# Row projections that start with a pair of chunks, 512 columns wide, split by the inner dimension

## The chip, the cores and the metric

The kernel runs on one core of a Trainium2 chip. A core has a matrix engine (TensorE, "PE" in the rows; its loads of the stationary operand are "PEld"), VectorE ("DVE"), ScalarE ("ACT"), GpSimd ("POOL") and SyncE ("SP"), which issues the transfers. Each engine runs its own list of instructions in order and waits on semaphores. The metric is the device time of one execution in microseconds (us); the time of the kernel before is the median of three runs.

## The reference, cut to what matters

Two transformer blocks follow one another on 256 rows of width 1024. The first block is applied for two layers, and each layer begins with a projection of the normed rows; a second one closes the attention. The second block has a cross attention whose output is projected in the same way.

```
for l in range(DEPTH):                      # 2 layers
    proj = h @ w_in[l]                      # (256 x 1024) @ (1024 x 1536)
    ... two attentions -> oa, ob ...
    mix = jnp.concatenate([oa, ob], axis=-1) @ w_o[l]      # 1024 x 1024
    h = layer_norm(DEEPNORM_ALPHA * h + mix, ln1_g[l], ln1_b[l])
    h = layer_norm(DEEPNORM_ALPHA * h + peer_ffn(h, ...), ...)
# second block: ... cross attention, its output @ w_o_x, rmsnorm, residual ...
```

So there are five such projections: w_in and w_o of layer 0, w_in and w_o of layer 1, and w_o_x. All data is float32.

## The kernel before, in words

**How a product is computed.** A float32 product is made of three products of rounded parts: high x high, high x low and low x high. The rows (the stationary operand) are turned by TensorE in two tiles of 128 rows (t = 0, 1), in eight blocks of 128 of the inner dimension each; ScalarE copies the turned tile from PSUM rounded to `xh` (the highs of the rows), and VectorE subtracts that copy to get `xl` (the lows). The copies are made by halves of a tile, four inner blocks each: `xh_half[t][i]` says that half i of tile t is there.

**Chunks.** A weight matrix comes in chunks of 256 columns with all 1024 rows, 1 MB each. SyncE loads them into the two places of `ring` in turn; a place is free again when both engines that read it have said so (`chunk_free`). A chunk has four quarters q; in the kernel before a quarter holds two inner blocks of 256 columns. ScalarE makes the high part of a quarter (`high`, L1415, into `wh`), once TensorE has left that quarter of `wh` (`parts_free[q]`). GpSimd makes the low parts of quarters 0 to 2 (`low`, L510, into `wl`), VectorE that of quarter 3 (`low`, L2103). `parts_ready[q]` tells TensorE.

**The start of a projection.** `to_xT` (L702) turns tile 0, computes some products whose result nobody reads (`spin`, L700, and `spin_on_weights`, L709, which keep the engine busy), turns tile 1, and spins again. `first_rows` (L743) then computes chunk 0: all high x high products first (16 matmuls of 256 columns, L752), then quarter by quarter the others (32 matmuls, L762). `rows_by_chunk` (L817) computes chunk 1 and the later ones, 12 matmuls of 256 columns (L829) per quarter, 48 per chunk; the last chunk of w_o and w_o_x is computed tile by tile (`rows_by_tile`, L839). Chunks alternate between two PSUM slots of two banks each, one bank per tile.

**The other engines.** ScalarE's list at a start is: the four highs of chunk 0, the four half copies of the turned tiles (`halves_to_xT`, L1493), then the highs of chunk 1 and so on. VectorE's list is: the four lows of the rows (`halves_low_xT`, L2137), `low(0, 3)`, and then for each chunk its low quarter and the taking of the result: a copy for w_in (L2212), a scaled add to the residual with statistics for w_o (L2342, L2346), a copy with sums of squares and a product with the gain for w_o_x (`residual_rows`, L1994, L1967, L2006). The kernel is one hand-written list per engine; nothing reorders it. Chunk 2 is loaded by `stream` (L313) once place 0 of the ring is free.

Of the kernel before, what the change touches and what calls it, by code (L numbers as in the profile page):

```python
# [8 lines left out]
P = 128  # L9
# [4 lines left out]
TT = S // P  # L14
HD = 64
CW = 256
CHUNK = KB * CW
N_IN, N_O, N_WQ = 6, 4, 8
# [24 lines left out]
def build(nc, A, out):  # L43
# [4 lines left out]
    with ctx:  # L48
# [633 lines left out]
        def _(pe):  # L682
# [60 lines left out]
            def first_rows(full):  # L743

                pe.wait_ge(slot_free[0], 1)
                pe.sem_inc(slot_free[0], -1)
                for t in range(TT):
                    for q in range(4):
                        if q % 2 == 0:
                            xh_in(t, q // 2)  # L750
                        for k in range(2):
                            pe.matmul(PS[:, t, 0:CW], xh[:, 2 * q + k, t * P:(t + 1) * P],  # L752
                                      wh[:, q, k * CW:(k + 1) * CW], start=q + k == 0, stop=False)
                for q in range(4):
                    if q % 2 == 0:
                        xl_in(q // 2)
                    pe.wait_ge(parts_ready[q], 1)
                    pe.sem_inc(parts_ready[q], -1)
                    for t in range(TT):
                        for k in range(2):  # L760
                            for i, (x, w) in enumerate(((xl, wh), (xh, wl))):
                                last = pe.matmul(PS[:, t, 0:CW], x[:, 2 * q + k, t * P:(t + 1) * P],  # L762
                                                 w[:, q, k * CW:(k + 1) * CW], start=False, stop=q + k + i == 5)
                    if q < 3:
                        last.then_inc(parts_free[q], 1)
                last.then_inc(full[0], 1)
# [219 lines left out]
            for l in range(DEPTH):  # L986

                to_xT(h, 11 if l else 0, 5 if l else 0, between=1 if l else 0, last=2 if l else 0)
# [13 lines left out]
                chunks(N_IN - 2, first_rows, rows_by_chunk, dve_full)  # L1002
# [847 lines left out]
        def _(dve):  # L1850
# [133 lines left out]
            def residual_rows(at, after, apart=False):  # L1984
# [11 lines left out]
                for c in range(3):  # L1996
# [204 lines left out]
            for l in range(DEPTH):  # L2201
# [4 lines left out]

                def take_proj(c):
                    at = (3 + c) % N_IN * CW
                    if 0 < c < 4:
                        low(c % 2, 3)  # L2210
# [9 lines left out]
                for c in range(3):  # L2220
                    take_proj(c)
# [835 lines left out]
```

## Time and profile before

| | |
|---|---|
| median of 3 runs | 2506.39 us (2502.34 to 2509.07) |
| the profiled execution | 2505.94 us, its span 2504.1 us |
| TensorE busy | 2412.5 us (96%) |
| VectorE busy | 1748.9 us (70%) |
| ScalarE busy | 1343.7 us (54%) |
| GpSimd busy | 709.0 us (28%) |
| mean granted TensorE clock | 0.994 |

Busy time of TensorE is counted with overlapping matmuls, so the share says that something is nearly always in the array, not that it runs at its peak. The waits that matter are short, some tenths of a microsecond each, and stand in the timeline of a few starts and ends of projections. The five starts lie at 16, 130, 1016, 1129 and 2261 us.

### The profile page before, as it was taken

Reading aid. Unit: us, or ns where it says so; the run is one execution under the profiler, and the core shown is the slowest. Engines: PE = TensorE matmul, PEld = TensorE weight load, DVE = VectorE, ACT = ScalarE, POOL = GpSimd, SP = SyncE. Lnnn points to the kernel's source line nnn. Section 1 sums busy time; section 2 is a strip of 40 time slices with the busy share of each in tenths; the row PEclk is TensorE's granted clock in tenths of the full one; section 3 lists DMA queues with packets and bytes.
Section 4 is the critical chain, followed back from the end, with each engine's and each line's share of the span. In section 5 each row is a group of like instructions: output and inputs, shape, how many; then the busy total and the mean of one; then the engine's idle time right before and its main releaser. Section 6 shows DMA issues by size and latency. Waiting matters only on the chain. (4 is left out here: it accounts for less than half of the span.)

```text
span 2504.1 us, 57329 instructions
## 1 busy us (share of the span) xinstructions
PE 2412.5 (96%) x16509; PEld 2211.3 (88%) x16509; DVE 1748.9 (70%) x3945; ACT 1343.7 (54%) x2396; POOL 709.0 (28%) x564
## 2 busy tenths in 40 slices
PE   6999999999999999999999999999999999899998
PEld 6899999999888888889999999988888887688996
DVE  5647777887677777554777788777777767556346
ACT  3545555776555555454555567655555543444443
POOL 5665444000000000566544400000000043134665
PEclk9999999999999999999999999999999999999999
DMA  6244566444566666623466644456666644333554
GB/s 239 85 153 168 210 230 226 168 152 180 177 245 236 246 236 243 237 85 137 167 217 225 228 164 161 174 182 241 241 241 242 243 157 158 142 135 110 174 186 152
DMA packets 98053, 475.31 MB, mean 190 GB/s; under 512 B 11808, under 2 KB 13344, under 8 KB 50720
## 3 DMA queue, kind: packets, MB, share of 16 engines
q1 hardware_dynamic: 97392, 472.91, 53.3%
q10 hardware_dynamic: 560, 1.19, 0.1%
q8 instruction: 46, 0.75, 0.1%
q14 instruction: 55, 0.45, 0.1%
HBM read 438.41 MB, written 35.65 MB: 189 GB/s over the span
## 5 line engine op out<-in xcount | busy, mean ns | idle before, releaser
L1415 ACT ACTIVATE wh<-ring 128x512 fp32r<-128x512 f32 x1428 | 881.9, 627 | 613.9 <-ACTq L1414 609.3
L2103 DVE TENSOR_TENSOR wl<-ring,wh 128x512 fp32r<-128x512 f32 x961 | 674.1, 707 | 273.0 <-DVEq L2102 254.2
L1100 PE MATMUL PS<-xh,wh 128*128 128x256 f32 x2048 | 593.6, 290 | 9.7 <-PEq L1096 8.2
L1100 PE MATMUL PS<-xl,wh 128*128 128x256 f32 x2048 | 579.6, 283 | 0.0
L1100 PE MATMUL PS<-xh,wl 128*128 128x256 f32 x2048 | 579.5, 283 | 0.0
L510 POOL TENSOR_TENSOR wl<-ring,wh 128x512 fp32r<-128x512 f32 x295 | 390.8, 1349 | 289.1 <-POOLq L509 287.3
L895 PE MATMUL PS<-wh,xh 128*128 128x512 f32 x1088 | 425.2, 391 | 2.5 <-PEq L892 2.5
L895 PE MATMUL PS<-wh,xl 128*128 128x512 f32 x1088 | 423.5, 389 | 0.0
L895 PE MATMUL PS<-wl,xh 128*128 128x512 f32 x1088 | 423.3, 389 | 0.0
L1100 PEld LDWEIGHTS PS<-xh,wh 128*128 128x128 f32 x2048 | 392.3, 192 | 15.3 <-issue 14.6
L1100 PEld LDWEIGHTS PS<-xl,wh 128*128 128x128 f32 x2048 | 392.9, 192 | 0.0
L1100 PEld LDWEIGHTS PS<-xh,wl 128*128 128x128 f32 x2048 | 392.3, 192 | 0.0
L496 POOL TENSOR_TENSOR rstd<-ve,mhalf 128x1 f32<-128x1 f32 (+3 forms) x30 | 31.2, 1039 | 1237.7 <-POOLq L495 1213.3
L636 POOL TENSOR_TENSOR wl<-ring,wh 128x512 fp32r<-128x512 f32 x144 | 205.7, 1430 | 230.4 <-POOLq L635 229.9
L895 PEld LDWEIGHTS PS<-wh,xh 128*128 128x128 f32 x1088 | 204.2, 188 | 49.3 <-issue 7.3
L895 PEld LDWEIGHTS PS<-wh,xl 128*128 128x128 f32 x1088 | 204.2, 188 | 42.7
L895 PEld LDWEIGHTS PS<-wl,xh 128*128 128x128 f32 x1088 | 204.3, 188 | 42.1 <-issue 0.5
L870 PE MATMUL PS<-xh,wh 128*128 128x256 f32 x688 | 196.9, 286 | 3.3 <-PEq L866 3.0
L870 PE MATMUL PS<-xl,wh 128*128 128x256 f32 x688 | 194.6, 283 | 0.0
L870 PE MATMUL PS<-xh,wl 128*128 128x256 f32 x688 | 194.5, 283 | 0.0
L1636 ACT ACTIVATE stg<-PS 128x256 f32<-128x256 f32 x256 | 97.9, 382 | 155.7 <-ACTq L1631 93.0
L1702 ACT ACTIVATE xh<-gains 128x256 fp32r<-128x256 f32 x248 | 103.6, 418 | 127.3 <-ACTq L1700 124.8
(339 smaller groups left out, 3826.5 us busy)
## 6 DMA issues: line engine op xcount, KB each, us to landing
ring<-in_peer_u SPq DMA_DIRECT2D x128, 1024.0 KB, 4.8
ring<-in_peer_v SPq DMA_DIRECT2D x128, 1024.0 KB, 4.8
acts<-stg SPq DMA_DIRECT2D x124, 256.0 KB, 2.1
gains<-acts SPq DMA_DIRECT2D x124, 256.0 KB, 4.9
ring<-in_w_in SPq DMA_DIRECT2D x24, 1024.0 KB, 4.9
ring<-in_w_gate_up SPq DMA_DIRECT2D x22, 1024.0 KB, 4.8
ring<-in_peer_wq SPq DMA_DIRECT2D x16, 1024.0 KB, 4.8
ring<-in_w_down SPq DMA_DIRECT2D x11, 1024.0 KB, 4.9
```

Source lines behind the costliest of these rows:

```text
L496: pool.tensor_tensor(rstd[:, at:at + n], ve[:, at:at + n], mhalf[:, :].to_broadcast([P, n]), ALU.pow).then_inc(rstd_ready, 1)
L510: part = pool.tensor_tensor(wl[:, q, :], ring[:, s, q * QW:(q + 1) * QW], wh[:, q, :].bitcast(F32), SUB)
L636: pool.tensor_tensor(wl[:, q, :], ring[:, s, q * QW:(q + 1) * QW], wh[:, q, :].bitcast(F32), SUB).then_inc(parts_ready[q] if q == 0 else p ...
L870: last = pe.matmul(PS[:, 2 * s + b, 0:S], w[:, q, k * CW + b * P:k * CW + (b + 1) * P], x[:, 2 * q + k, :], start=q + k + i == 0, stop=q + ...
L895: last = pe.matmul(acc[:, t, c * 512:(c + 1) * 512], (xh, xl)[x][:, at + j, t * P:(t + 1) * P], w[:, q, :], start=begin and j + i == 0, st ...
L1100: last = pe.matmul(PS[:, 2 * j, 0:S], w[:, q, k * P:(k + 1) * P], x[:, at, :], start=at + i == 0, stop=at + i == 9)
L1415: act.activation(wh[:, q, :], ring[:, s, q * QW:(q + 1) * QW], ACT.Copy).then_inc(high_ready[q], 1)
L1636: last = act.activation(stg[:, s, j * S:(j + 1) * S], PS[:, 2 * j, 0:S], ACT.Gelu)
L1702: act.activation(wst[0][:, j, :], buf[:, j * S:(j + 1) * S], ACT.Copy).then_inc(cast_ready[j], 1)
L2103: part = dve.tensor_tensor(wl[:, q, :], ring[:, s, q * QW:(q + 1) * QW], wh[:, q, :].bitcast(F32), SUB)
```

## The change

The first two chunks of the five projections become a pair. The host lays their weights out anew (`first_pair_wide`): the first chunk of the pair now holds inner blocks 0 to 3 with 512 columns, one block per quarter, the second chunk inner blocks 4 to 7. `wide_start` takes the place of `to_xT`, `first_rows` and `rows_by_chunk` for chunk 1. It writes 512 columns per tile into the slot 1.

```
+            def wide_start(src, idle=0, spins=(0, 0, 0), halves=True):
...
+                def highs(t):
+                    xh_in(t, 0)
+                    for q in range(4):
+                        pe.matmul(PS[:, 2 + t, :], xh[:, q, t * P:(t + 1) * P], wh[:, q, :], start=q == 0, stop=False)
...
+                turn(0, 0)
+                turn(0, 1)
+                pe.wait_ge(highs_in, 1)
...
+                spin_on_weights(spins[0])
+                pe.wait_ge(slot_free[1], 1)
...
+                highs(0)
+                spin_on_weights(spins[1])
...
+                turn(1, 0)
+                spin_on_weights(spins[2])
+                highs(1)
+                turn(1, 1)
...
                 for q in range(4):
...
+                        for x, w in ((xl, wh), (xh, wl)):
+                            last = pe.matmul(PS[:, 2 + t, :], x[:, q, t * P:(t + 1) * P], w[:, q, :], start=False,
+                                             stop=False)
+                    last.then_inc(parts_free[q], 1)
+                for t in range(TT):
+                    xh_in(t, 1)
+                    pe.wait_ge(slot_free[2 + t], 1)
+                for q in range(4):
...
+                        for i, (x, w) in enumerate(((xh, wh), (xh, wl), (xl, wh))):
+                            last = pe.matmul(PS[:, 2 + t, :], x[:, 4 + q, t * P:(t + 1) * P], w[:, q, :], start=False,
+                                             stop=q == 3 and i == 2)
...
-                to_xT(h, 11 if l else 0, 5 if l else 0, between=1 if l else 0, last=2 if l else 0)
+                wide_start(h, 11 if l else 0, (1, 1, 1) if l else (0, 0, 0))
...
-                to_xT(o_all, 14, 6, halves=False, last=2)
-                first_rows(dve_full)
-                rows_by_chunk(1, dve_full)
+                wide_start(o_all, 14, (1, 1, 1), False)
...
-            to_xT(o_all, 0, 2, halves=False, last=2)
-            first_rows(dve_full)
-            rows_by_chunk(1, dve_full)
+            wide_start(o_all, 0, (1, 0, 1), False)
```

VectorE takes the pair in one operation. For w_o the order of low and statistics changes too:

```
-                for i in range(3):
-                    s = i % 2
-                    if i:
-                        low(s, 3)
+                low(1, 3)
+                for s, lo, hi in ((1, 0, 2), (0, 2, 3)):
                     take_rows(s)
...
                     dve.sem_inc(slot_free[s], 1)
+                    low(1 - s, 3)
                     for t in range(TT):
-                        dve.bn_stats(stats4[:, t, i, :], h[:, t, c])
-                low(1, 3)
+                        for i in range(lo, hi):
+                            dve.bn_stats(stats4[:, t, i, :], h[:, t, CW * i:CW * (i + 1)])
```

For w_o_x the pair is copied (1024 columns in all), then come `low(0, 3)`, two sums of squares of 512 columns, and one product with the gain of 1024 columns; chunk 2 and the last one are taken as before. For w_in the pair is copied in one operation.

**What moves on TensorE, at the start of w_o.** The names: `ident` turns, `PS<-wh` alone is a spin, `wh,xh` is high x high. Before:

```order
L726 MATMUL PS<-ident,arena 128x128 [waits slot_free2,src_ready]
L726 MATMUL PS<-ident,arena 128x128 x7
L709 MATMUL PS<-wh 128x512 [waits highs_in,slot_free0]
L709 MATMUL PS<-wh 128x512 x5
L726 MATMUL PS<-ident,arena 128x128 [waits slot_free3,src_ready]
L726 MATMUL PS<-ident,arena 128x128 x7
L709 MATMUL PS<-wh 128x512 x2
L752 MATMUL PS<-wh,xh 128x256 [waits slot_free0,xh_half00]
L752 MATMUL PS<-wh,xh 128x256 x3
L752 MATMUL PS<-wh,xh 128x256 [waits xh_half01]
```

The same place in the changed kernel:

```order
L750 MATMUL PS<-ident,arena 128x128 x7
L761 MATMUL PS<-wh 128x512 [waits highs_in]
L757 MATMUL PS<-wh,xh 128x512 [waits slot_free1,xh_half00]
L757 MATMUL PS<-wh,xh 128x512 x3
L761 MATMUL PS<-wh 128x512
L750 MATMUL PS<-ident,arena 128x128 [waits slot_free3,src_ready]
L750 MATMUL PS<-ident,arena 128x128 x3
L761 MATMUL PS<-wh 128x512
L757 MATMUL PS<-wh,xh 128x512 [waits xh_half10]
L757 MATMUL PS<-wh,xh 128x512 x3
L750 MATMUL PS<-ident,arena 128x128 x4
L791 MATMUL PS<-wh,xl 128x512 [waits xl_half0,xl_half1,parts_ready0]
```

Four products of each tile now stand between the turns, and the second half of tile 1 is turned behind the products of its first half.

**What moves on VectorE, in w_o behind the start.** `L2342` and `L2392` add the result to the residual, `BN_STATS` are the statistics, `wl<-ring,wh` is the low quarter. Before, from chunk 1's low quarter to that of the last chunk:

```order
L2103 TENSOR_TENSOR wl<-ring,wh 128x512 [waits high_ready3]
L2342 SCALAR_TENSOR_TENSOR h<-h,PS 128x2x256 [waits dve_own,dve_full1]
L2346 BN_STATS stats<-h 128x6 [waits dve_own]
L2346 BN_STATS stats<-h 128x6
L2103 TENSOR_TENSOR wl<-ring,wh 128x512 [waits high_ready3]
L2342 SCALAR_TENSOR_TENSOR h<-h,PS 128x2x256 [waits dve_own,dve_full0]
L2346 BN_STATS stats<-h 128x6 [waits dve_own]
L2346 BN_STATS stats<-h 128x6
L2103 TENSOR_TENSOR wl<-ring,wh 128x512 [waits high_ready3]
```

In the changed kernel:

```order
L2152 TENSOR_TENSOR wl<-ring,wh 128x512 [waits dve_own,high_ready3]
L2392 SCALAR_TENSOR_TENSOR h<-h,PS 128x2x512 [waits dve_own,dve_full1]
L2152 TENSOR_TENSOR wl<-ring,wh 128x512 [waits dve_own,high_ready3]
L2398 BN_STATS stats<-h 128x6 [waits dve_own]
L2398 BN_STATS stats<-h 128x6 x3
L2392 SCALAR_TENSOR_TENSOR h<-h,PS 128x2x256 [waits dve_full0]
L2152 TENSOR_TENSOR wl<-ring,wh 128x512 [waits dve_own,high_ready3]
L2398 BN_STATS stats<-h 128x6 [waits dve_own]
```

The last chunk's low quarter now stands ahead of the statistics of chunk 2. On VectorE in w_o_x, from the pair's copy to the last chunk's low quarter, the changed kernel has:

```order
L2037 COPY arena<-PS 128x2x512 [waits dve_own,dve_full1]
L2152 TENSOR_TENSOR wl<-ring,wh 128x512 [waits dve_own,high_ready3]
L2004 ISA arena,stats<-arena 128x512 [waits dve_own]
L2004 ISA stats 128x1
L2042 MEMSET stats 128x1
L2004 ISA arena,stats<-arena 128x512
L2044 TENSOR_TENSOR arena<-arena,gains 128x2x512 [waits dve_own]
L2031 COPY arena<-PS 128x2x256 [waits dve_full0]
L2004 ISA arena,stats<-arena 128x256 [waits dve_own]
L2152 TENSOR_TENSOR wl<-ring,wh 128x512 [waits high_ready3]
```

Before, the work on chunk 0 was spread over the time in which chunk 1 was computed; now all of the pair's stands between the end of the pair and that of chunk 2. The order of instructions on ScalarE, GpSimd and SyncE is unchanged.

## Rows read from the trace of the kernel before

**Rows 1.** Page, part 1: busy time and its share of the span.

```profile
PE 2412.5 (96%) x16509; PEld 2211.3 (88%) x16509; DVE 1748.9 (70%) x3945; ACT 1343.7 (54%) x2396; POOL 709.0 (28%) x564
```

**Rows 2.** Timeline, TensorE, w_o of layer 0: start, duration, engine, line, operation, count.

```profile
136.22 0.28 PE L762 MATMUL PS<-wh,xl 128*128 128x256 f32 x1
...
140.06 0.29 PE L829 MATMUL PS<-wh,xh 128*128 128x256 f32 x1
```

**Rows 3.** Timeline, TensorE: 512 columns in the expert stage, 53 matmuls apart.

```profile
1929.79 0.39 PE L895 MATMUL PS<-wh,xl 128*128 128x512 f32 x1
...
1941.80 0.39 PE L895 MATMUL PS<-wl,xh 128*128 128x512 f32 x1
```

**Rows 4.** Timeline, TensorE, the start of w_o in layer 0.

```profile
132.93 1.07 PE L726 MATMUL PS<-ident,arena 128*128 128x128 f32 x8 [0.50 <-PEq L724]
...
134.30 2.08 PE L752 MATMUL PS<-wh,xh 128*128 128x256 f32 x16
```

**Rows 5.** Timeline, ScalarE, the same stretch.

```profile
130.73 1.09 ACT L1493 ACTIVATE xh<-PS 128x512 fp32r<-128x512 f32 x2 [2.10 <-ACTq L1492]
133.69 1.09 ACT L1493 ACTIVATE xh<-PS 128x512 fp32r<-128x512 f32 x2 [1.86 <-ACTq L1492]
137.47 0.63 ACT L1415 ACTIVATE wh<-ring 128x512 fp32r<-128x512 f32 x1 [2.69 <-ACTq L1414]
...
142.23 0.63 ACT L1415 ACTIVATE wh<-ring 128x512 fp32r<-128x512 f32 x1 [1.10 <-ACTq L1414]
```

**Rows 6.** Timelines, VectorE and GpSimd, the same stretch.

```profile
134.43 1.89 DVE L2137 TENSOR_TENSOR xl<-PS,xh 128x512 fp32r<-128x512 f32 x3 [1.04 <-PEq L733]
136.23 0.68 DVE L2103 TENSOR_TENSOR wl<-ring,wh 128x512 fp32r<-128x512 f32 x1
...
143.04 3.80 POOL L510 TENSOR_TENSOR wl<-ring,wh 128x512 fp32r<-128x512 f32 x3 [0.98 <-POOLq L509]
```

**Rows 7.** SyncE's issue of chunk 2, and its line's time to landing.

```profile
137.26 0.33 SPq L319 DMA_DIRECT2D ring<-in_w_o  x1
...
DMA to landing us min/median/max: 4.8/4.8/4.8
```

**Rows 8.** Timelines, VectorE and TensorE, the end of w_o in layer 0.

```profile
152.91 0.75 DVE L2346 BATCH_NORM_STATS2 stats<-h 128x6 f32<-128x256 f32 x2 [0.24 <-DVEq L1855]
153.58 0.67 DVE L2103 TENSOR_TENSOR wl<-ring,wh 128x512 fp32r<-128x512 f32 x1
...
154.55 0.36 PE L851 MATMUL PS<-wh,xh 128*128 128x256 f32 x1 [0.66 <-PEq L847]
```

**Rows 9.** Timeline, the start of w_in in layer 0.

```profile
21.45 2.88 PE L752 MATMUL PS<-wh,xh 128*128 128x256 f32 x16
...
24.16 0.28 PE L762 MATMUL PS<-wh,xl 128*128 128x256 f32 x1
...
24.81 11.70 SPq L319 DMA_DIRECT2D ring<-in_w_in  x3
```

**Rows 10.** Timeline, the start of w_in in layer 1.

```profile
1019.76 2.08 PE L752 MATMUL PS<-wh,xh 128*128 128x256 f32 x16
...
1019.12 4.25 POOL L510 TENSOR_TENSOR wl<-ring,wh 128x512 fp32r<-128x512 f32 x3 [2.91 <-POOLq L509]
...
1023.85 16.71 SPq L319 DMA_DIRECT2D ring<-in_w_in  x4
```

**Rows 11.** Timeline, w_o_x: its start on TensorE and ScalarE, its last low quarter on VectorE.

```profile
2262.63 1.06 PE L726 MATMUL PS<-ident,arena 128*128 128x128 f32 x8
...
2261.75 1.09 ACT L1493 ACTIVATE xh<-PS 128x512 fp32r<-128x512 f32 x2 [1.22 <-ACTq L1492]
...
2283.46 0.68 DVE L2103 TENSOR_TENSOR wl<-ring,wh 128x512 fp32r<-128x512 f32 x1
```

**Rows 12.** One line of the kernel: product with the gain; duration ns min/median/max.

```profile
L2006 DVE TENSOR_TENSOR arena<-arena,gains x3: 692/1541/1680, 2274.6 to 2285.1; 128x512 f32<-128x512 f32 x3
```

**Rows 13.** Busy time by stretches: length, PE, PEld, DVE, ACT, POOL, clock, DMA.

```profile
1115.00:1120.00 5.00, 4.78 (x29) 4.81 (x29) 2.13 (x4) 2.18 (x3) 3.67 (x3) 0.66 0.01 3
```

More of the change, by code:

```diff
@@ L759, in first_rows @@
                     for t in range(TT):
[L760 to L763, printed above, removed]
+                        for x, w in ((xl, wh), (xh, wl)):
[6 more added lines that the diff above has]
+                for q in range(4):
+                    pe.wait_ge(parts_ready[q], 1)
+                    pe.sem_inc(parts_ready[q], -1)
+                    for t in range(TT):
+                        for i, (x, w) in enumerate(((xh, wh), (xh, wl), (xl, wh))):
+                            last = pe.matmul(PS[:, 2 + t, :], x[:, 4 + q, t * P:(t + 1) * P], w[:, q, :], start=False,
+                                             stop=q == 3 and i == 2)
                     if q < 3:
                         last.then_inc(parts_free[q], 1)
-                last.then_inc(full[0], 1)
+                last.then_inc(dve_full[1], 1)
             def first_cols(full):
@@ L1994, in taken @@
                         own(dve.tensor_copy(dst, PS[:, 2 * s + t0:2 * s + t1, 0:CW]))
-                for c in range(3):
+                if not apart:
+                    low(1, 3)
+                    take_rows(1)
+                    c = slice(0, 2 * CW)
+                    own(dve.tensor_copy(o_all[:, :, c], PS[:, 2:4, :]))
+                    dve.sem_inc(slot_free[1], 1)
+                    low(0, 3)
+                    for t in range(TT):
+                        sum_of_squares(o_all[:, t, c], t, sums4[:, t, 0:1])
+                        dve.memset(sums4[:, t, 1:2], 0.0)
+                    own(dve.engine_nop())
+                    dve.tensor_tensor(o_all[:, :, c], o_all[:, :, c], bc(g[:, c].unsqueeze(1), TT, 2 * CW), MUL)
+                for c in range(0 if apart else 2, 3):
                     s, cols = c % 2, slice(CW * c, CW * (c + 1))
@@ L2218, in values_of @@
                                     proj[:, :, at:at + 128].rearrange("p t (g d) -> p t g d", g=2))
-                for c in range(3):
-                    take_proj(c)
+                take_proj(2)
                 own(dve.engine_nop())
@@ L3004, in layout @@
     w = x["w_in"][:, :, cols]
-    a["w_in"] = np.stack([by_chunk(m) for m in w])
+    a["w_in"] = np.stack([first_pair_wide(by_chunk(m)) for m in w])
     pairs = np.array([HD * i + j for i in PAIRS for j in range(HD)])
     both = np.concatenate([pairs, 512 + pairs])
-    a["w_o"] = np.stack([by_chunk(m[both]) for m in x["w_o"]])
+    a["w_o"] = np.stack([first_pair_wide(by_chunk(m[both])) for m in x["w_o"]])
     a["peer_wq"] = np.stack([by_chunk(m) for m in x["peer_wq"]])
@@ L3036, in layout @@
     a["w_out_2"] = by_chunk(x["w_out_2"][np.concatenate([np.arange(512), 512 + pairs])])
-    for n in ("w_q_x_2", "w_kv_x_2", "w_o_x_2"):
+    for n in ("w_q_x_2", "w_kv_x_2"):
         a[n] = by_chunk(x[n])
+    a["w_o_x_2"] = first_pair_wide(by_chunk(x["w_o_x_2"]))
     w = x["w_gate_up_2"]
```

47 lines of the change are left out of this document (33 added, 14 removed).

## The prediction

> **What bounds the kernel now.** I read the page's busy times first: TensorE is busy for 96% of the span [rows 1], so the time changes only where TensorE's list gets shorter or waits less. Then I took the timelines of the five starts, each engine by itself, because the change touches nothing else. The reader is to see in them a chain of four engines that delivers chunk 2. I write L for the moment at which the first product with a low part begins.
>
> In w_o of layer 0, L is 136.22 [rows 2]. From there the kernel before has 80 matmuls of 256 columns until chunk 2 (32 of chunk 0, 48 of chunk 1). 32 of them take 140.06 - 136.22 = 3.84 us, 0.120 each [rows 2], so chunk 2 begins at 136.22 + 9.60 = 145.8. Its weights come by another way: VectorE's last low of the rows and `low(0, 3)` end at 136.91 [rows 6], the transfer is issued at 137.26 and takes 4.8 [rows 7], ScalarE begins the first quarter at 142.23 [rows 5], which is 4.97 behind the issue, GpSimd follows at 143.04 and needs 3.80/3 = 1.27 for a quarter [rows 6]. With 0.1 for the signal to TensorE (my estimate, from the steps of 0.1 to 0.2 between such rows) the first quarter is ready at 144.4. So this way has 1.4 us to spare. The change uses that up.
>
> **Part 1, wider matmuls.** 53 matmuls of 512 columns take 12.01 us, 0.2266 each [rows 3], against 2 x 0.120 = 0.240 [rows 2]. 48 wide ones in place of 96 save 48 x 0.0134 = 0.64 us of TensorE per start, 3.2 for the five. Both rows are of this kernel's kind of operand, each matmul with its own stationary load, so I take the value and no range.
>
> Here the Trainium skill ("TensorE: Matmul & The Clock Gate", "Wait — 56ns, not 53.3ns?") would speak against the change: it gives a matmul at the full clock as columns over 2.4 GHz plus about 2.5 ns, so widening would save only that 2.5 ns per pair, 0.1 us per start. By the rows the constant part is 13 ns (0.120 us for 256 columns, 0.2266 for 512), and the rows decide. By the page the own-work terms below would each be 0.5 smaller.
>
> **Part 2, products between the turns, w_o.** In the changed kernel of w_o, layer 0: the first half of tile 0 is copied at 130.73 + 0.60 = 131.33 [rows 5]; four wide products run from 131.43 to 132.34, one spin to 132.57. Tile 1 can be turned at 132.93 as before, when VectorE delivers it [rows 4]. Its first half is copied from 133.69 to 134.29 [rows 5], the next four products take 134.37 to 135.28, the other four turns (8 take 1.07 with their tail, so about 0.115 each [rows 4]) end at 135.74. That is the new L: 0.48 earlier. Of the 48 wide matmuls 40 are left, 9.06 us; TensorE alone would begin chunk 2 at 144.8, 1.0 us earlier.
>
> But the second half of tile 1 is now turned behind products. Its copy begins 0.76 behind the turn (as 133.69 stands to 132.93 [rows 4, 5]), at 136.04, ends at 136.64; VectorE's last low of the rows and `low(0, 3)` (0.60 and 0.68 [rows 6]) end at 138.0 instead of 136.91. The transfer goes out 1.1 us later; everything behind it moves along: issue 138.35, ScalarE 143.3, GpSimd 144.1, ready 145.5. Chunk 2 begins at 145.5: a gain of 0.3 instead of 1.0, and TensorE stands for 0.7 us in a new wait, at the first quarter of chunk 2. Chunk 1's own quarters are just in time: `parts_free[0]` comes 0.68 + 0.39 behind L, ScalarE 0.12 and 0.63, GpSimd 0.18 and 1.27 later, ready at L + 3.4; TensorE wants it at L + 16 x 0.2266 = L + 3.63. Behind GpSimd's wait nothing else is queued there.
>
> **Part 3, the low quarter ahead of the statistics, w_o.** TensorE waits in the last chunk for its low quarter: 154.55 [rows 8], while 18 matmuls behind the chunk's begin it could have gone on at about 153.7. VectorE does the statistics from 152.91 to 153.58 and only then the quarter [rows 8]. The change swaps them: 0.67 us earlier, of a wait of 0.8. What is late next is the same quarter, by 0.1. So w_o gains 0.3 + 0.67, about 1.0, and twice that for two layers: -1.9 (bounds per layer -0.2, where the transfer comes still later, and -1.6, where it doesn't bind).
>
> **Part 4, w_in of layer 1.** Here GpSimd starts late, at 1019.12, and ends chunk 0's third quarter at 1023.37; the transfer at 1023.85 waits for that [rows 10], not for VectorE. In the changed kernel VectorE is through at 1023.55 by the same steps as above, so the transfer stays where it is, and so does the first quarter of chunk 2: 1023.85 + 4.97 + 0.81 + 1.27 + 0.1 = 1031.0. Before, chunk 2 began at 1019.76 + 1.92 + 9.60 = 1031.3 [rows 10]. Gain 0.3 (bounds 0 and 0.7, TensorE's own).
>
> **Part 5, w_in of layer 0.** TensorE still runs at the lower of its two levels (1.2 GHz): 16 matmuls took 2.88 us here [rows 9], 2.08 in the other starts [rows 4]. Four wide products cost 1.7 us there, not 0.9. The list before turned both tiles without a product between; now the eight products come first. I get highs(0) from 20.2 to 21.9, the turn, its copy by 23.7, highs(1) to 24.7 (if the clock has risen) and L at 25.4 instead of 24.16 [rows 9]. The transfer, 24.81 before [rows 9], waits for the last low of the rows: about 28.0. Ready at 28.0 + 7.15 (4.97, 0.81, 1.27 and 0.1 as above) = 35.15; before, chunk 2 began at 24.16 + 9.6 = 33.8. Loss 1.4 (bounds 0.8, TensorE alone, and 2.4 with highs(1) at the low level too).
>
> **Part 6, w_o_x.** Nothing keeps tile 1 waiting here: it was turned at 2262.63 [rows 11]. Now it stands behind highs(0), which needs the copy of 2261.75 + 0.60 [rows 11] and ends at 2263.34. All later steps move: L' 2266.13, transfer 2268.75, first quarter ready at 2275.9; before, chunk 2 began at 2262.63 + 12.9 = 2275.5 (as 145.8 stands to 132.93 in w_o). That is +0.4. Then VectorE's work on the pair: copy 1.2, low 0.7, two sums of squares 0.7 each, product 1.2, 4.7 with the gaps, starting 0.5 behind the pair's end (2275.2): done at 2280.4, in time for chunk 2's end at 2281.7. But it runs beside GpSimd: the product of 512 columns takes 0.69 alone and 1.54 to 1.68 there [rows 12]. Three such operations cost up to 2.8 more, 2283.2, and then the last chunk's low quarter (2283.46 before [rows 11]) is 1.0 later still. The value: half of that, so +1.0 in all (bounds -0.4 and +2.2).
>
> On this the Trainium skill ("SBUF — State Buffer", "SBUF: two separate sides") says that VectorE operations with two SBUF inputs and GpSimd share a port pair as an exclusive lock, held for a whole instruction. The rows agree; its bound, one GpSimd operation of 1.27 waited for by each of the three, would make the excess 3.8 instead of 2.8.
>
> **The sum.** +1.4 (w_in, 0) - 1.9 (w_o, twice) - 0.3 (w_in, 1) + 1.0 (w_o_x) = +0.2. On the profiled execution (2505.94, span 2504.1 and 1.8 around it) that gives 2506.1; it lies 0.45 under the median of the runs, so on the median I forecast 2506.6. The sum of the good bounds is 0.8 - 3.2 - 0.7 - 0.4 = -3.5, of the bad ones 2.4 - 0.4 + 0 + 2.2 = +4.2: 2502.9 to 2510.8. The runs of before scatter from -4.1 to +2.7 around their median. A change under 0.3% (7.5 us) is what a measurement here can't tell from none.
>
> **Rivals.** (a) *TensorE's own work decides.* The transfer isn't what chunk 2 waits for, because it lands sooner (there is less traffic) or GpSimd is quicker than I add up. Then the good bounds hold: 2503. For it: the way has 1.4 us to spare today. Against: my steps are the rows' own. Only if the turns too cost nothing, 1.9 per start and 0.7 twice for part 3, would it be 10 us, 2496.
>
> (b) *Slower: the clock falls.* Before, six to eight fillers per start stand around the turns; now two or three do, with gaps of some tenths in front of the second products (133.8 to 134.4). If the granted clock falls to 1.2 GHz in the starts, a fall costs what it cost elsewhere: a clock of 0.66 over 5 us [rows 13], 3.4 us at half speed, 1.7 of work. In all four later starts 6.8 us: 2513.4, and more where the slow stretch lasts into the pair. It decides from the point where the gaps, not the products, fill a start. Against: products of data replace the fillers nearly one for one (eight wide ones).
>
> (c) *GpSimd is late inside the pair.* The slack of 0.2 at chunk 1's first quarter goes if its operation takes 1.43 as it does beside VectorE (4.25 / 3 [rows 10]); some 0.5 per start on top: 2509.
>
> **Chances.** The forecast 0.66, (a) 0.18, (b) 0.08, (c) 0.08. The range goes from 2500, (a) with the scatter, to 2512, (c) with it and the start of (b). Faster by over 0.3% (under 2498.9) needs the far end of (a): 0.07. Slower (over 2513.9) needs (b): 0.07. Within: 0.86.
>
> **What would show it.** In the changed profile: wide matmuls 0.2266 apart; L near 135.7 in w_o of layer 0; TensorE idle about 0.7 us in front of chunk 2 in w_o, waiting for GpSimd; the transfer of chunk 2 some 1.1 us later; no idle time above 0.2 at the last low quarter of w_o; chunk 2 of the first w_in 1.4 us later; in w_o_x VectorE's product with the gain at over 2 us and chunk 2 taken late. I am wrong if chunk 2 follows the pair without a gap, if the granted clock dips at a start, or if a stage outside the five moves by more than 1 us.

## The result, and the profile after

The changed kernel takes 2511.48 us (median of 18 runs, 2507.04 to 2513.97), the kernel before 2506.95 us (18 runs, 2501.61 to 2509.79). The ratio is 1.0019, with a 95% interval of 1.0011 to 1.0026: 4.5 us longer. The time lies in the forecast range and within 0.3%, but the sum of the terms was +0.2, and 4.5 is even a little over the sum of the bad bounds, +4.2. Some terms were mis-sized, and the rest of this document says which.

The busy shares hardly move (the row answers to [rows 1]):

```profile
PE 2410.3 (96%) x16252; PEld 2194.4 (88%) x16252; DVE 1754.8 (70%) x3937; ACT 1343.0 (54%) x2396; POOL 708.9 (28%) x564
```

I measure each of the five stages from its first turn to the next stage's first turn. Behind w_o and w_o_x that is the whole projection; in w_in it is the turn that follows the fourth of its six chunks. The whole is a median; the stages are from the profiled execution of each kernel.

| stage | before | after | difference | forecast |
|---|---|---|---|---|
| w_in, layer 0 | 30.15 | 33.46 | +3.3 | +1.4 |
| w_o, layer 0 | 32.13 | 31.57 | -0.56 | -0.95 |
| w_in, layer 1 | 27.07 | 27.55 | +0.5 | -0.3 |
| w_o, layer 1 | 32.54 | 31.69 | -0.85 | -0.95 |
| w_o_x | 33.01 | 35.89 | +2.9 | +1.0 |
| sum | 154.90 | 160.16 | +5.3 | +0.2 |

The spans differ by 3.3 (2507.4 against 2504.1), so the two profiles also differ by -2.0 outside the five stages; more on that at the end. The 5.3 of the stages and the 4.5 of the medians don't contradict each other: the interval of the ratio is 2.8 to 6.5 us.

TensorE at the start of w_o, layer 0, in the changed kernel (it answers to [rows 2, 4]; columns as there):

```profile
132.59 1.04 PE L750 MATMUL PS<-ident,arena 128*128 128x128 f32 x8
...
134.06 1.17 PE L757 MATMUL PS<-wh,xh 128*128 128x512 f32 x4 [0.20 <-PEq L733]
...
135.51 0.63 PE L750 MATMUL PS<-ident,arena 128*128 128x128 f32 x4
...
137.01 1.16 PE L757 MATMUL PS<-wh,xh 128*128 128x512 f32 x4 [0.64 <-PEq L733]
138.01 0.60 PE L750 MATMUL PS<-ident,arena 128*128 128x128 f32 x4
138.36 0.48 PE L791 MATMUL PS<-wh,xl 128*128 128x512 f32 x1
...
148.31 0.36 PE L869 MATMUL PS<-wh,xh 128*128 128x256 f32 x1 [0.49 <-PEq L864]
```

L comes 5.77 behind the first turn; before it was 136.22 - 130.01 = 6.21. But the last four turns stand at +5.42, behind tile 2's products (I count the tiles 1 and 2 here; they are t = 0 and 1 in the code), and chunk 2 has a new wait of 0.49. ScalarE, VectorE and SyncE of the same stretch (answering to [rows 5 to 7]) show what feeds that wait:

```profile
136.27 0.60 ACT L1530 ACTIVATE xh<-PS 128x512 fp32r<-128x512 f32 x1 [1.86 <-ACTq L1529]
138.73 0.60 ACT L1530 ACTIVATE xh<-PS 128x512 fp32r<-128x512 f32 x1 [1.87 <-ACTq L1529]
...
139.48 0.69 DVE L2186 TENSOR_TENSOR xl<-PS,xh 128x512 fp32r<-128x512 f32 x1 [1.18 <-DVEq L2184]
140.09 0.68 DVE L2152 TENSOR_TENSOR wl<-ring,wh 128x512 fp32r<-128x512 f32 x1
...
141.11 4.53 SPq L319 DMA_DIRECT2D ring<-in_w_o  x2
```

Last turn, copy (138.73), last low of the rows (139.48), `low(0, 3)` (140.09), transfer (141.11): each starts as the one ahead ends. The transfer stands at +8.52; it was at 137.26 - 130.01 = +7.25 [rows 7].

The end of w_o, on VectorE (answering to [rows 8]): the low quarter now stands ahead of the statistics, and TensorE goes on without a wait that the profile marks.

```profile
155.58 0.69 DVE L2152 TENSOR_TENSOR wl<-ring,wh 128x512 fp32r<-128x512 f32 x1 [0.35 <-DVEq L2151]
156.60 0.76 DVE L2398 BATCH_NORM_STATS2 stats<-h 128x6 f32<-128x256 f32 x2 [0.33 <-DVEq L1892]
```

TensorE and SyncE at w_in of layer 0 (answering to [rows 9]):

```profile
15.20 1.94 PE L750 MATMUL PS<-ident,h 128*128 128x128 f32 x8 [15.20 <-PEq L748]
19.14 2.04 PE L757 MATMUL PS<-wh,xh 128*128 128x512 f32 x4 [2.01 <-PEq L733]
20.99 1.05 PE L750 MATMUL PS<-ident,h 128*128 128x128 f32 x4
22.91 2.04 PE L757 MATMUL PS<-wh,xh 128*128 128x512 f32 x4 [0.87 <-PEq L733]
24.75 1.05 PE L750 MATMUL PS<-ident,h 128*128 128x128 f32 x4
25.46 0.78 PE L791 MATMUL PS<-wh,xl 128*128 128x512 f32 x1
...
28.17 0.43 PE L791 MATMUL PS<-wh,xl 128*128 128x512 f32 x1
...
35.94 0.28 PE L869 MATMUL PS<-wh,xh 128*128 128x256 f32 x1
...
28.48 5.19 SPq L319 DMA_DIRECT2D ring<-in_w_in  x2
```

Both groups of products take 2.04 instead of 1.17, and six more wide matmuls, from 25.46 to 28.17, take 0.45 each instead of 0.2266. L is at +10.26; before it was at 24.16 - 16.34 = +7.82. Chunk 2 follows the pair at 35.94 without a wait. (Everything starts 1.14 earlier here than before. That is not the change: two other profiles with the same order at this start, e4 and e5 below, begin at 16.16 and 16.58.)

The low level is read from these durations. The column of the granted clock gives 1.00 for this stretch all the same (length, PE, PEld, DVE, ACT, POOL, granted clock, DMA):

```profile
20.00:25.00 5.00, 4.13 (x13) 2.87 (x13) 1.50 (x3) 0.60 (x1) 1.19 (x1) 1.00 0.89 310
```

w_in of layer 1 (answering to [rows 10]): chunk 2 waits, and its transfer goes out at 1026.02 - 1017.53 = +8.49 instead of +7.90.

```profile
1033.30 0.36 PE L869 MATMUL PS<-wh,xh 128*128 128x256 f32 x1 [0.75 <-PEq L864]
...
1026.02 0.34 SPq L319 DMA_DIRECT2D ring<-in_w_in  x1
```

w_o_x on TensorE and VectorE (answering to [rows 11, 12]):

```profile
2278.46 0.36 PE L869 MATMUL PS<-wh,xh 128*128 128x256 f32 x1 [0.74 <-PEq L864]
...
2289.30 0.36 PE L891 MATMUL PS<-wh,xh 128*128 128x256 f32 x1 [2.07 <-PEq L887]
...
2277.96 1.23 DVE L2037 COPY arena<-PS 128x1024 f32<-128x1024 f32 x1 [3.06 <-DVEq L2145]
2279.53 1.83 DVE L2152 TENSOR_TENSOR wl<-ring,wh 128x512 fp32r<-128x512 f32 x1 [0.35 <-DVEq L2151]
2281.73 1.41 DVE L2004 CUSTOM_DVE_ANT_0 arena<-arena 128x512 f32<-128x512 f32 x1 [0.37 <-DVEq L1892]
...
2283.08 1.77 DVE L2004 CUSTOM_DVE_ANT_0 arena<-arena 128x512 f32<-128x512 f32 x1
...
2285.02 2.07 DVE L2044 TENSOR_TENSOR arena<-arena,gains 128x1024 f32<-128x1024 f32 x1 [0.15 <-DVEq L1892]
2287.01 0.68 DVE L2031 COPY arena<-PS 128x512 f32<-128x512 f32 x1
...
2288.32 0.69 DVE L2152 TENSOR_TENSOR wl<-ring,wh 128x512 fp32r<-128x512 f32 x1
```

Chunk 2 ended at about 2284.3 on TensorE and was taken at 2287.01, because VectorE was still at the pair. TensorE then stood 2.07 us for the low quarter of 2288.32.

### The profile page after: what moved, and what is told of

It reads as the page before. It is cut to its first block and busy times, and to the rows that moved or that the text cites. A ratio compares the mean times of both kernels' runs of the same rounds, so it can differ in the third digit from the quotient of the medians.

```text
span 2507.4 us, 56773 instructions
## 1 busy us (share of the span) xinstructions
PE 2410.3 (96%) x16252; PEld 2194.4 (88%) x16252; DVE 1754.8 (70%) x3937; ACT 1343.0 (54%) x2396; POOL 708.9 (28%) x564
```

## The experiments

My theory was that the loss has separate causes: a low clock at the first start, VectorE's pair work in w_o_x, a late transfer elsewhere. The rivals were that the width costs, or that the interleaving costs everywhere. All stages, in us, from the profile of each kernel; "time" is the median of its runs (10 to 12 of each experiment), "ratio" sets it against the kernel before, measured beside it, with its interval:

| kernel | w_in 0 | w_o 0 | w_in 1 | w_o 1 | w_o_x | sum | time | ratio |
|---|---|---|---|---|---|---|---|---|
| before | 30.15 | 32.13 | 27.07 | 32.54 | 33.01 | 154.9 | 2506.95 | |
| after | 33.46 | 31.57 | 27.55 | 31.69 | 35.89 | 160.2 | 2511.48 | 1.0019 (1.0011 to 1.0026) |
| e1 | 30.10 | 31.59 | 27.48 | 31.59 | 35.78 | 156.5 | 2507.11 | 1.0003 (0.9993 to 1.0013) |
| e2 | 32.20 | 31.70 | 27.51 | 31.74 | 33.13 | 156.3 | 2507.64 | 1.0008 (0.9999 to 1.0018) |
| e3 | 31.12 | 31.59 | 27.08 | 31.97 | 32.99 | 154.8 | 2503.97 | 0.9991 (0.9982 to 1.0000) |
| e4 | 33.58 | 30.81 | 26.62 | 30.76 | 34.08 | 155.9 | 2509.72 | 1.0014 (1.0003 to 1.0025) |
| e5 | 33.49 | 31.63 | 27.48 | 31.53 | 34.37 | 158.5 | 2512.65 | 1.0027 (1.0015 to 1.0039) |
| e6 | 29.91 | 31.07 | 26.74 | 31.01 | 33.46 | 152.2 | 2504.91 | 0.9998 (0.9988 to 1.0008) |
| e7 | 30.74 | 30.72 | 26.75 | 30.90 | 33.63 | 152.7 | 2507.51 | 1.0002 (0.9993 to 1.0011) |
| e8 | 33.33 | 31.58 | 28.22 | 31.75 | 38.56 | 163.4 | 2508.94 | 1.0009 (1.0000 to 1.0019) |
| e9 | 31.52 | 30.40 | 27.03 | 30.46 | 34.40 | 153.8 | 2505.27 | 0.9996 (0.9987 to 1.0005) |
| e10 | 30.53 | 31.02 | 26.68 | 31.10 | 33.03 | 152.4 | 2504.81 | 0.9998 (0.9989 to 1.0007) |
| e11 | 30.21 | 30.74 | 27.03 | 30.53 | 33.16 | 151.7 | 2504.47 | 0.9994 (0.9985 to 1.0003) |
| e12 | 29.56 | 30.40 | 26.75 | 30.40 | 33.03 | 150.1 | 2504.50 | 0.9992 (0.9983 to 1.0001) |

A stage that an experiment doesn't touch repeats within 0.2 us, except w_in of layer 0 (up to 1.3, e2 against after), where the clock rises at different moments, and two stages of e8: w_o_x (below) and w_in of layer 1, 0.7 more than after. There chunk 2's transfer goes out as in after (+8.46 against +8.49), but ScalarE begins its first quarter 5.76 us behind the issue instead of 5.05; why the transfer took longer is open. So the stages tell tenths apart (w_in of layer 0 only some 1.3), the whole some 2 us.

**e1: the old order at the first start.**

```diff
-                wide_start(h, 11 if l else 0, (1, 1, 1) if l else (0, 0, 0))
+                wide_start(h, 11 if l else 0, (1, 1, 1) if l else (0, 0, 0), turned=l == 0)
...
+                if turned:
+                    turn(1, 0)
+                    turn(1, 1)
+                    highs(0)
+                    highs(1)
...
```

> The changed kernel, with the old order at the first start of w_in alone: both tiles turned, then the high products of both, still 512 columns wide. From the first turn to the first turn of proj (L694) that stage took 30.15 us before and 33.46 after. Theory (TensorE still runs at its low level there, and each piece of product put in front of a turn of the second tile holds back ScalarE, VectorE and the first low product, which came 10.26 after the first turn instead of 7.82): the first low product comes at +7.8 to +8.4, the stage takes 30.8 to 31.6, the whole 2508.6 to 2509.8. Rival (the width, the pair's one copy and its later release cost it): the stage stays within 0.5 of 33.4, the whole at 2511.5.

Measured: 30.10 and 2507.11 us. On TensorE:

```profile
20.20 3.17 PE L757 MATMUL PS<-wh,xh 128*128 128x512 f32 x8
23.21 0.39 PE L804 MATMUL PS<-wh,xl 128*128 128x512 f32 x1
```

L is at +8.12 and at the high level's pitch, as the theory has it; the stage is even 0.7 under its range. So the loss of this stage is the order and not the width. Its size is less sure than 3.3, because the moment of the clock's rise moves both sides: over all profiles the stage takes 29.56 to 31.12 us where both tiles are turned first (before, e1, e3, e6, e7, e10, e11, e12), and 32.20 to 33.58 in the four that have after's order and nothing else at this start (after, e2, e4, e5). In the shortest of those four, e2, the high level is there already at tile 2's products (first turn at 15.25):

```profile
22.95 1.16 PE L757 MATMUL PS<-wh,xh 128*128 128x512 f32 x4 [0.87 <-PEq L733]
...
24.31 0.48 PE L791 MATMUL PS<-wh,xl 128*128 128x512 f32 x1
```

**e2: w_o_x as before.** Its start, chunk layout and VectorE order are those of the kernel before.

```diff
-            wide_start(o_all, 0, (1, 0, 1), False)
+            to_xT(o_all, 0, 2, halves=False, last=2)
+            first_rows(dve_full)
+            rows_by_chunk(1, dve_full)
...
```

> The changed kernel with w_o_x as it was before (chunks of 256 columns, turns first, VectorE's old order). That stage took 33.02 us from its first turn to the next stage's first turn before, 35.89 after. Theory (the change costs 2.9 us in this stage, by VectorE's pair work ahead of the last quarter's rest): back to 33.0 to 33.3, the whole at 2508.3 to 2509.0. Rival (the stage only inherits something of the ones before it, such as the transfers' or GpSimd's place): 35 to 36, and the whole stays at 2511.5.

Measured: the stage 33.13, as expected; the whole 2507.64, 0.7 under its range. The 2.9 us are made in this stage.

**e4: the low quarter ahead of the last low of the rows.**

```diff
             def halves_low_xT(early=False):
...
+                        if early and i and t:
+                            low(0, 3)
```

> The changed kernel, with VectorE's rest of the last quarter of the first half placed ahead of the last of the four rests of rows, at all five starts, so that chunk 2's transfer is released earlier. Theory (the transfer of chunk 2 is released by that rest alone, GpSimd being done 4 us before, and TensorE waits 0.49 to 0.75 us for it): at w_o the transfer starts 6.3 to 6.8 us after the first turn instead of 8.5, the wait ahead of chunk 2 is under 0.2 us at the four later starts, each of these is 0.4 to 0.8 shorter, the whole 2508.8 to 2510. Rival (what is behind it, ScalarE's highs or VectorE's take of the pair, comes just as late): the waits shrink by less than 0.2, the whole stays within 1 us of 2511.5.

Measured: the transfers at w_o stand at +6.64 and +6.68, no wait ahead of chunk 2 is left in the four later starts, and the stages (w_o 0, w_in 1, w_o 1, w_o_x) are 0.77, 0.93, 0.93 and 1.8 shorter than after. The whole, 2509.72, is only 1.8 under after, within what such a comparison can tell. So what VectorE does behind the last turn is what set chunk 2.

**e5: the pair's gain in w_o_x behind chunk 2.**

```diff
-                    dve.tensor_tensor(o_all[:, :, c], o_all[:, :, c], bc(g[:, c].unsqueeze(1), TT, 2 * CW), MUL)
...
+                    if not apart:
+                        cols = slice(0, 3 * CW)
```

> The changed kernel; in w_o_x VectorE's product of the pair with the gain goes behind the take of chunk 2, in one operation with that of chunk 2 (768 columns of both tiles), so that chunk 2 is taken and the last quarter's rest made about 2.1 us earlier. Theory (the 2.07 us for which TensorE waited in front of chunk 3's last quarter is that product): the wait falls below 0.3, the stage takes 34.0 to 34.6 instead of 35.89, the whole 2509.7 to 2510.3. Rival (VectorE has more work there than TensorE has products, in whatever order): the wait goes over to the take of the last tile and the stage stays above 35.4.

Measured: the stage 34.37, as the theory has it, and the wait of 2.07 is gone. The whole didn't follow: 2512.65. The stages say 1.7 under after, the runs say 1.2 over; what lies outside the stages isn't resolved.

**e3: the kernel before, with the swap on VectorE alone.**

```diff
-                    if i:
-                        low(s, 3)
...
                     dve.sem_inc(slot_free[s], 1)
+                    low(1 - s, 3)
                     for t in range(TT):
                         dve.bn_stats(stats4[:, t, i, :], h[:, t, c])
-                low(1, 3)
```

> The kernel before, with one thing of the change: at w_o of both layers VectorE makes the rest of the next chunk's last quarter ahead of the statistics of h and not behind them. The stage (first turn to the next stage's first turn) took 32.13 and 32.54 us before, 31.57 and 31.69 after. Theory (this swap alone carries w_o's gain; the wide pair and the new order of turns give it nothing, since chunk 2 starts no earlier): 31.2 to 31.6 and 31.4 to 31.8, the whole 2504.6 to 2505.4 against 2506.6. Rival (the gain is the earlier first low product, and VectorE's order is hidden): 32.0 to 32.2 and 32.4 to 32.6, the whole unchanged.

Measured: 31.59 and 31.97 us, 0.54 and 0.57 less than before. In layer 0 that is all of what the changed kernel gains at w_o (0.56), in layer 1 two thirds of it (31.97 is over the expected range). The whole is 2503.97, the lowest of all, but its interval (0.9982 to 1.0000) touches the kernel before.

**e6: wide, but both tiles turned first, everywhere.** The fillers are those of the kernel before.

```diff
-            def wide_start(src, idle=0, spins=(0, 0, 0), halves=True):
+            def wide_start(src, idle=0, spins=(0, 0, 0), halves=True, turned=True):
...
-                wide_start(o_all, 14, (1, 1, 1), False)
+                wide_start(o_all, 14, (6, 0, 2), False)
...
```

> The changed kernel with both tiles turned ahead of every product at all five starts, and with the counts of filling products of the kernel before; the pair is 512 columns wide still. This is the width without the interleaving. Stages after: w_in 33.46 and 27.55, w_o 31.57 and 31.69, w_o_x 35.89; before: 30.15, 27.07, 32.13, 32.54, 33.01. Theory (at the first start the interleaving costs, at the others it gives some tenths that the wait ahead of chunk 2 takes back; w_o_x pays for the pair's VectorE work): w_in 30.1 and 27.4 to 28.0, w_o 31.5 to 32.0 twice, w_o_x 35.8 to 36.5; the whole 2507 to 2508.5. Rival (the interleaving holds back the second tile's rests everywhere, and with them chunk 2): w_in 30.1 and 26.9, w_o 30.9, w_o_x under 34.5; the whole under 2505.

The rival stands and my theory falls: the stages are 29.91, 31.07, 26.74, 31.01 and 33.46. Against after, without the interleaving, they are 3.6, 0.5, 0.8, 0.7 and 2.4 us shorter, 8.0 together; the whole is 2504.91, 6.6 under after. (The number of fillers differs as well; e1, e4 and e9, which leave it alone, show that it is not what counts at w_in and w_o. At w_o_x that isn't separated.) TensorE and SyncE at w_o, layer 0 (first turn at 128.77):

```profile
131.69 1.06 PE L750 MATMUL PS<-ident,arena 128*128 128x128 f32 x8 [0.51 <-PEq L748]
...
134.89 0.39 PE L804 MATMUL PS<-wh,xl 128*128 128x512 f32 x1
...
143.96 0.28 PE L882 MATMUL PS<-wh,xh 128*128 128x256 f32 x1
...
136.01 0.33 SPq L319 DMA_DIRECT2D ring<-in_w_o  x1
```

L is later than after (+6.12 against +5.77), but the transfer goes out at +7.24, and chunk 2 follows the pair without a wait at +15.19 (after: +15.72). At this w_o e6 is 1.06 under before: 0.54 of it is the swap (e3), 0.52 is left for the width, against 0.64 by TensorE's rows.

**e7: e1, e4 and e5 together.**

> The changed kernel with three edits together: turns first at the first start of w_in alone (took 3.36 off there), VectorE's rest of the last quarter ahead of the last rest of rows at all five starts (took 0.8, 0.9 and 0.9 off w_o, w_o and w_in of layer 1, 1.8 off w_o_x), and the gain of w_o_x in one operation behind the take of chunk 2 (took 1.5 off). Theory (they lie at different places and add up): w_in 30.1 and 26.6, w_o 30.8 twice, w_o_x 32.5 to 33.2; the sum of the five is 4.0 below the kernel before, the whole 2502 to 2503.5. Rival (what two of them take off w_o_x is the same wait; and waits outside of the five stages give part back): w_o_x 34.0, the whole 2504 to 2506.

Measured: the first four stages are up to 0.6 over the expected values (30.74, 30.72, 26.75, 30.90), w_o_x 33.63, between theory and rival. The late product of 768 columns takes 1.76 us on VectorE and stands in front of the take of the last chunk's first tile, so part of the gain comes back there, as the rival has it. The whole is 2507.51; the sum of the stages had promised 2.2 under before, and the measurement doesn't show it.

**e8: TensorE busy ahead of the first turn.**

```diff
             pe.wait_ge(consts_pe, 1)
             pe.sem_inc(consts_pe, -1)
+            for _ in range(64):
+                pe.transpose(ps2(0)[:, 0:P], ident[:, :], ident[:, :])
```

> The changed kernel, with 64 transposes of the identity by itself ahead of the first turn, so that TensorE, which waits there for the layer norm from 3 to 15 us, comes to w_in at its high level. Nothing else is changed. Stage w_in of layer 0 took 33.46 us (30.10 with turns first). Theory (the 3.3 us are the pieces of product that TensorE does at its low level between the turns, 2.04 for four instead of 1.17): the eight turns take 1.0 instead of 1.94, the first low product comes at +6.0 to +7.0 instead of +10.26, the stage takes 28.0 to 29.3, the whole 2506.5 to 2507.5. Rival (the second tile's turns come late because of the layer norm and the chain of the engines behind it, at whatever clock): the first low product at +8.5 or later, the stage above 31.

Neither number of the theory came: L at +10.06, the stage 33.33. These are the rival's numbers, but its reason (at whatever clock) isn't shown by them, since the clock did not stay high. TensorE, and the busy time by stretches (length, PE, PEld, DVE, ACT, POOL, granted clock, DMA):

```profile
15.33 1.06 PE L750 MATMUL PS<-ident,h 128*128 128x128 f32 x8 [1.41 <-PEq L748]
19.39 1.73 PE L757 MATMUL PS<-wh,xh 128*128 128x512 f32 x4 [3.00 <-PEq L733]
20.92 1.05 PE L750 MATMUL PS<-ident,h 128*128 128x128 f32 x4
22.84 2.04 PE L757 MATMUL PS<-wh,xh 128*128 128x512 f32 x4 [0.87 <-PEq L733]
```

```profile
10.00:15.00 5.00, 3.92 (x36) 3.68 (x34) 2.38 (x2) 0.04 (x1) 0.00 (x0) 1.00 0.98 385
15.00:20.00 5.00, 1.68 (x10) 1.43 (x11) 4.16 (x5) 4.52 (x7) 2.94 (x2) 0.97 0.15 64
20.00:25.00 5.00, 4.13 (x13) 2.90 (x12) 1.62 (x3) 0.60 (x1) 1.32 (x2) 0.50 0.87 306
```

The first turns now run at the high level (1.06 for eight), but in front of tile 1's products TensorE stands 3.0 us for ScalarE's copies, and the granted clock falls to 0.50, the 1.2 GHz level. So the low clock here isn't only the start of the program: TensorE came to it anew out of a wait. The extra work in front bought nothing, because the wait behind it was long enough to lose it again; the granted clock from 25 to 30 is still 0.84.

**e9: only the last turn put back ahead of tile 2's products.**

```diff
                 spin_on_weights(spins[2])
+                turn(1, 1)
                 highs(1)
-                turn(1, 1)
```

> The changed kernel with one exchange: the second half of tile 2's turns stands ahead of tile 2's high products and not behind them, at all five starts. Tile 1's products still stand ahead of tile 2's turns. Theory (the delay of the very last turn, from which ScalarE's copy, VectorE's last rest of rows, its rest of the last quarter and so the transfer of chunk 2 follow, is what the interleaving costs at the four later starts): at w_o this turn comes at +3.5 instead of +5.42, chunk 2 is requested at +7.0 to +7.4 instead of +8.52, the wait ahead of chunk 2 is under 0.15; the stages take 30.6 to 31.2, 26.6 to 27.1, 30.6 to 31.2 and 34.0 to 35.0 (w_o, w_in of layer 1, w_o, w_o_x) instead of 31.57, 27.55, 31.69 and 35.89, and w_in of layer 0 some 1.5 to 3 less than 33.46; the whole 2505.5 to 2508. Rival (what costs is that tile 2's first turns stand behind tile 1's products): the waits ahead of chunk 2 stay over 0.3 and the stages within 0.3 of the changed kernel's.

Measured: 31.52, 30.40, 27.03, 30.46 and 34.40 us, the whole 2505.27. At w_o (first turn at 131.62):

```profile
135.24 0.60 PE L750 MATMUL PS<-ident,arena 128*128 128x128 f32 x4
136.03 1.16 PE L757 MATMUL PS<-wh,xh 128*128 128x512 f32 x4 [0.20 <-PEq L733]
137.05 0.47 PE L791 MATMUL PS<-wh,xl 128*128 128x512 f32 x1
...
146.24 0.29 PE L869 MATMUL PS<-wh,xh 128*128 128x256 f32 x1
...
138.86 0.33 SPq L319 DMA_DIRECT2D ring<-in_w_o  x1
```

One exchange of two calls gives both: L at +5.43 and the transfer at +7.24, so chunk 2 starts at +14.62, 1.1 earlier than after. This is the direct test of the last turn. Against e6 it leaves 0.9 at w_o_x and 1.6 at the first start, where tile 1's products still stand ahead of tile 2's turns, and at w_in of layer 1 a wait of 0.48 (the theory had under 0.15) and 0.3. At w_o it is 0.6 shorter than e6: there tile 1's products in front of tile 2's turns help.

**e10: e6, with the gain of w_o_x in two operations.**

> The wide pair with both tiles turned first at all five starts (this took 29.91, 31.07, 26.74, 31.01 and 33.46 us for the five stages), and in w_o_x the gain of the pair in two operations: tile 1's ahead of the take of chunk 2, tile 2's behind the rest of chunk 3's last quarter. TensorE waited 1.39 us for that rest. Theory (the product of 2.07 us on VectorE holds it back, and a product of one tile takes about 0.7 to 1.0): the wait falls to 0.2 to 0.6, w_o_x takes 32.4 to 33.0, the other stages stay, the whole 2502.5 to 2504.5 (before 2506.8). Rival (VectorE's chain behind the last tile sets the end, and what is put off comes back there): w_o_x 33.3 to 33.8, the whole 2504 to 2505.5.

Measured: 33.03, at the upper end; the wait is 0.86. The product of one tile took 1.53 us beside GpSimd, not 0.7 to 1.0. The whole is 2504.81, in the rival's range.

**e11: e10, with tile 1's products in the gap at w_o and at w_in of layer 1, without the last filler.**

> As the run with the pair's gain in two operations, but at w_o of both layers and at w_in of layer 1 tile 1's high products stand in the gap in front of tile 2's turns, in place of the filling products, and all of tile 2's turns together behind them. At w_o tile 2's data come 2.9 us after the first turn, and tile 1's products would be done by 2.7. Theory (products that end before the turns' data are there cost nothing and bring the first low product forward): first low product at w_o at +5.2 to +5.6 instead of +6.12, the last turn no later than +3.6, the stage 30.2 to 30.7 instead of 31.07 and 31.01, w_in of layer 1 26.4 to 26.8; the whole 2501.5 to 2503.5. Rival (chunk 2 or a later transfer becomes the bound, so the tenths are given back): waits ahead of chunk 2 of 0.3 or more and stages of 31.0.

Measured: 30.74 and 30.53 at w_o, 27.03 at w_in of layer 1. The theory holds at w_o, the rival at w_in, where chunk 2 waits 0.49: there tile 2 is ready early and nothing is to be had from the gap. The whole is 2504.47, 1.0 over the expected range.

**e12: each start in its shortest order (w_o as in e9, the others as in e10).**

> The wide pair at all five starts; each start in the order that was shortest so far: at w_in of both layers and at w_o_x both tiles turned ahead of every product (29.9 to 30.7, 26.7 and, with the pair's gain in two operations, 33.0 us), at w_o of both layers tile 1's high products in the gap ahead of tile 2's turns and tile 2's behind them (30.4 and 30.5). Theory (the stages add up): 30.2, 30.4, 26.7, 30.5 and 33.1, together 4.0 us under the kernel before, the whole 2502 to 2503.5 against 2506.6, faster by 0.12 to 0.18 per cent. Rival (part of it is lost outside of the five stages, as in the run with three edits, whose stages summed to 2.2 us under before and whose time did not): 2504 to 2506.5.

Measured: 150.1 us for the five stages, 4.8 under before and 10.0 under after. The whole is 2504.50 against 2505.88: a ratio of 0.9992 (0.9983 to 1.0001). That is in the rival's range and not in the theory's: of the 4.8 us in the stages the whole shows 1.4 (2.0 by the ratio). The estimate is on the good side of the kernel before, and the interval still touches it; set against after by the two ratios, it is 0.27% or about 7 us shorter.

## Why the prediction came out as it did

The time was right within the range, but with luck: the three terms of w_in and w_o_x all came out beyond their bad bounds, and 2511.48 is inside only because the range reaches beyond the sum of the bad bounds (given as 2510.8; 2506.4 + 4.2 is 2510.6), to 2512. By its own steps:

- **Wider matmuls, 0.64 us per start:** right. The wide matmuls stand 0.23 apart, and e6's w_o begins chunk 2 9.07 behind L instead of 9.6. The stage got 0.52 of the 0.64 there (e6 less e3), and in the changed kernel's first w_o nothing.
- **Interleaving at w_o, L 0.48 earlier, transfer 1.1 later, a new wait of 0.7:** right in each part. From the first turn, L came 0.44 earlier, the transfer 1.27 later, the wait was 0.49. But -0.3 per layer was 0 at the first one, where the transfer's delay ate all of it, and -0.3 at the second (0.85 less the 0.57 of the swap).
- **The low quarter ahead of the statistics, -0.67:** the mechanism was right, the size 0.54 and 0.57 (e3). The wait was taken as 0.8, where the row itself shows 0.66 of idle time.
- **w_in of layer 1, -0.3:** the sign was wrong (+0.5). The step that failed is "VectorE is through at 1023.55 by the same steps as above". Those steps were w_o's, where tile 2 comes late anyway. Here tile 2 was turned 2.21 behind the first turn before, and tile 1's products held it to 2.73, so VectorE and not GpSimd released the transfer, 0.6 later.
- **w_in of layer 0, +1.4, bounds 0.8 and 2.4:** +3.3. Up to the second copy the forecast holds. Then "highs(1) to 24.7 (if the clock has risen)" failed, and it failed further than the bad bound: the clock stayed low for highs(1), the last turns and six matmuls of the pair. The condition was named but not priced to its end. Whether it comes true is chance: in e2, the same code at this start, the clock had risen by highs(1), L came at +9.06, just where the forecast has it (25.4 - 16.34), chunk 2 waited 0.70 as forecast, and the stage was 2.05 over before, within the bounds. In after, e4 and e5 L came at +10.25 or +10.26. Whether the waits of this order hold the clock down longer than unbroken work does, these few profiles don't show.
- **w_o_x, +1.0, bounds -0.4 and +2.2:** +2.9. Two sizes were off. Chunk 2 came 0.97 later (forecast 0.4). And of the excess on VectorE I took half of 2.8. Measured against 0.69 for the low and for each sum and 1.2 for the product, the four operations took 1.14 + 0.72 + 1.08 + 0.87 = 3.8 us more. The three that were priced, the sums and the product, took 2.7 more, which is the 2.8 of the rows in full; the fourth, the low quarter, had been given no excess at all. The 3.8 worked out from the Trainium skill ("SBUF — State Buffer", "SBUF: two separate sides") is met only by coincidence, since it was for three operations; with its rule the trace agrees in that no single excess (0.72 to 1.14) is above one GpSimd operation of 1.27.
- **Rivals:** (a) didn't happen at the four later starts; at w_in of layer 0 chunk 2 did follow the pair without a wait, behind late products. Its condition can be made: with the last turn in time (e9) TensorE's own work does decide at w_o. (b) didn't happen in the changed kernel's four later starts. (c) didn't: chunk 1 follows without a wait.

What the prediction did not see is that most of the loss has one cause. Parts 2, 5 and 6 priced the delay of tile 2's chain each by itself, part 4 left it out, and the sum of the interleaving (8.0 us against e6) is larger than the gain of the width. Only at w_o_x does a second one stay: VectorE's work on the pair. With both tiles turned first (e6) TensorE still waits 1.39 for the low quarter there, and the stage is 0.45 over before.

## What to carry to other kernels

An operand that is wanted late can still gate early: ask of every instruction that is put in front of a turn, a copy or an evacuation who releases a buffer behind it, and follow that to the transfer that it lets go. Products may fill a gap in front of work whose data are late, as tile 1's do at w_o; they may not stand in front of work whose data are there. A wider evacuation puts more of the other engine's work in one place, and beside GpSimd that work took 1.7 to 2.7 times as long in the changed kernel (2.07 against 1.23 and 1.83 against 0.69). Price it in full; which operation is hit differs from run to run (in e5 the same low quarter took 0.69).

## What the runs showed of the hardware

- A wait on TensorE can bring the clock down at some times and not at others. In w_o_x the wait of 2.07 us left the granted clock at 1.00 in the changed kernel. In e8 the same wait was followed by two stretches at 0.62 and 0.70, and the stage took 2.7 us more:

```profile
2285.00:2290.00 5.00, 3.08 (x14) 3.11 (x15) 3.44 (x11) 0.05 (x1) 0.00 (x0) 0.62 0.35 103
2290.00:2295.00 5.00, 5.00 (x26) 4.69 (x25) 1.43 (x7) 2.46 (x4) 0.55 (x1) 0.70 0.27 110
```

  Here too the clock falls at a wait in one execution and not in the other, and what decides it is open. So rival (b) exists, behind a long wait; none of the short waits at the four later starts brought it.
- Outside the five stages the profiles differ by up to 13 us without an edit there (2344.7 in e8 to 2357.6 in e4, if each span is taken less its stages), and part of it is the granted clock. Between w_in and w_o of layer 1 most profiles show 83.5 to 83.9 us; before, e4, e11 and e12 show 84.9 to 86.7, and three of these have a stretch at 0.66 to 0.75 there (e4 has one at 0.77 from 1085 to 1090):

```profile
1115.00:1120.00 5.00, 5.00 (x31) 5.00 (x32) 1.85 (x3) 1.90 (x3) 3.68 (x3) 0.66 0.01 3
```

  This row is e12's; before has the same value [rows 13], the changed kernel 1.00. Both kernels wait ahead of the turns there (1.83 us before, 1.68 in the changed kernel). Between w_in and w_o of layer 1 before takes 2.3 us longer than the changed kernel, which accounts for the -2.0 outside the stages. Why it comes in some executions is left open.
